# Experts' matrices in one ring of five places, with context's work spread earlier over the experts

## The reference

```python
def expert_block(args):
    xb, e = args
    hdn = jax.nn.silu(xb @ w1[e]) * (xb @ w3[e])      # w1, w3: 1024 x 512, 32 experts
    return hdn @ w2[e]                                # w2: 512 x 1024
...
proj_c = hc @ w_ctx                                   # hc: the context, normed and modulated; w_ctx: 1024 x 2560
kc = rms_norm_2(proj_c[..., :GQA_KV_WIDTH].reshape(B, L, GQA_KV_HEADS, GQA_HEAD_DIM), p["k_norm"])
vc = proj_c[..., GQA_KV_WIDTH:GQA_CTX_COLS].reshape(B, L, GQA_KV_HEADS, GQA_HEAD_DIM)
...
oc = gqa_attend(qc, kc, vc).reshape(B, L, GQA_WIDTH)
yc = (oc * jax.nn.silu(gc)) @ p["w_out"]
```

## Time and profile before

| | us |
|---|---|
| median of 3 runs (lowest, highest) | 2011.4 (2009.6, 2015.0) |
| the profiled execution | 2020.8 |
| its span | 2018.7 |
| TensorE busy | 1821.2 (90% of the span) |
| VectorE, ScalarE busy | 753.6, 540.1 |
| DMA, mean over the span | 165 GB/s |
| the experts' loop, first SiLU to last output | 453 to 1025 |

### The profile page before, as it was taken

How to read it: one execution, slowest core, us unless ns; L and a number is a source line. 1 busy time by engine, 2 the same in 40 slices (tenths; PEclk the granted TensorE clock), 3 DMA queues, 4 the chain that set the end, 5 groups by cost and what they waited for, 6 DMA issues and landing times. The chain is left out here.

```text
span 2018.7 us, 24057 instructions
## 1 busy us (share of the span) xinstructions
PE 1821.2 (90%) x9644; PEld 1007.6 (50%) x9644; DVE 753.6 (37%) x1471; ACT 540.1 (27%) x1110; POOL 148.2 (7%) x194
## 2 busy tenths in 40 slices
PE   8999878988788989999869999899998999699998
PEld 3333455454344434446445444566645544466663
DVE  2333576131124111134323314566423225555542
ACT  2111476110110011133214212444311232234430
POOL 2110000000111101110000014000000001100000
PEclk9999899979898989999989999999998999899999
DMA  7655927249999999999671222000200011000001
GB/s 264 217 184 184 190 33 100 112 176 415 403 390 388 412 398 388 401 375 354 262 280 70 83 83 83 1 1 1 97 0 32 21 57 63 22 1 2 1 22 42
DMA packets 91950, 333.44 MB, mean 165 GB/s; under 512 B 10112, under 2 KB 26624, under 8 KB 64832
## 3 DMA queue, kind: packets, MB, share of 16 engines
q1 hardware_dynamic: 73376, 247.64, 34.8%
q10 hardware_dynamic: 13264, 67.22, 8.8%
q0 software_dynamic: 5200, 17.04, 2.1%
HBM read 317.58 MB, written 14.30 MB: 164 GB/s over the span
## 5 line engine op out<-in xcount | busy, mean ns | idle before, releaser
L1015 PE MATMUL mix_ps<-arena 128*64 128x256 f32 x2048 | 238.1, 386 | 2.5 <-DVE arena L1510 2.5
L2031 PE MATMUL tail_ps<-arena 128*128 128x512 f32 x504 | 219.6, 592 | 0.0
L1027 PE MATMUL mix_ps<-arena 128*64 128x512 f32 x512 | 145.2, 719 | 66.9 <-DMA arena<-in_w 66.3
L1015 PEld LDWEIGHTS mix_ps<-arena 128*64 128x64 f32 x2048 | 143.3, 138 | 89.1 <-issue 20.2
L903 PE MATMUL mix_ps<-arena,side 128*128 128x512 f32 x384 | 175.3, 609 | 1.4 <-DVE side L1335 1.4
L443 DVE TENSOR_REDUCE tail_small<-tail_ps 128x1 f32<-128x768 f32 x128 | 116.6, 953 | 137.7 <-PE tail_ps L327 137.7
L2031 PEld LDWEIGHTS tail_ps<-arena 128*128 128x128 f32 x504 | 95.0, 190 | 114.8 <-issue 114.3
L903 PEld LDWEIGHTS mix_ps<-arena,side 128*128 128x128 f32 x384 | 72.1, 194 | 103.4 <-issue 85.2
L2031 PE MATMUL tail_ps<-arena,side 128*128 128x512 f32 (+2 forms) x320 | 122.1, 543 | 0.0
L526 ACT ACTIVATE arena<-tail_ps,tail_small 128x768 f32<-128x768 f32 x128 | 113.8, 899 | 3.7 <-DVE tail_small L443 3.7
L1027 PEld LDWEIGHTS mix_ps<-arena 128*64 128x64 f32 x512 | 40.6, 164 | 147.6 <-issue 77.2
(11 more groups left out here) (373 smaller groups left out, 2323.7 us busy)
## 6 DMA issues: line engine op xcount, KB each, us to landing
arena<-in_w SPq DMA_DIRECT2D x66, 2048.0 KB, 12.0
arena<-in_w ACTq DMA_DIRECT2D x30, 2048.0 KB, 10.6
arena<-in_l_w_in SPq DMA_DIRECT2D x22, 1024.0 KB, 7.4
arena<-in_l_w_mod SPq DMA_DIRECT2D x16, 1024.0 KB, 5.0
arena<-in_w_in SPq DMA_DIRECT2D x12, 1024.0 KB, 9.3
arena<-in_l_w_mod SPq DMA_DIRECT2D x16, 512.0 KB, 4.5
residual<-bias_blocks SPq DMA_DIRECT2D x32, 224.0 KB, 10.1
arena<-in_l_w_out SPq DMA_DIRECT2D x6, 1024.0 KB, 5.1
```

The lines of the kernel that those rows point to most:

```text
L1015: last = pe.matmul(out[h * CAP:(h + 1) * CAP, 0:H2], x, wb[:, k, h * H2:(h + 1) * H2], start=(k == 0), stop=(k == DK - 1))
L1027: last = pe.matmul(py[h * CAP:(h + 1) * CAP, :], x, wb[:, f, h * 512:(h + 1) * 512], start=(f == 0), stop=(f == FK - 1))
L2031: last = pe.matmul(out, lhs(k), rhs(k), start=(k == 0), stop=(k == K - 1))
```

## The change

The five places become one ring for all three kinds of matrix, in the order in which TensorE uses them: w1(0), w3(0), then w1(e+1), w3(e+1), w2(e) and so on, so that use q lies in place q % 5 and may be loaded when use q - 5 is done. For w2(e) that is h1(e); ScalarE asks for it behind silu(e). SP asks for w1(e+2) when h3(e) is done and for w3(e+2) when second(e-1) is done. The six pieces of context's columns are asked for by ScalarE too, in experts 9, 11, ... 19. Context's product goes from experts 12 to 23 to experts 9 to 20, its steps from three an expert from 24 on to two an expert from 21 on, the small work on modulation, gates, side and overflow into experts 1 to 6. The three matrices of the last expert have places of their own in the ring. Two of the four "cg" pieces are loaded in the second block.

```diff
-    w1b = [view(proj_w, 0, DK, D_EXPERT), view(ring, SLOT, DK, D_EXPERT)]
-    w3b = [view(proj_w, 4096, DK, D_EXPERT), view(ring, 3 * SLOT, DK, D_EXPERT)]
-    w2b = view(proj_w, 8192, D_EXPERT // P, D)
+    matrix_at = [view(proj_w, 0, 4096), view(proj_w, 4096, 4096), view(ring, SLOT, 4096), view(ring, 3 * SLOT, 4096), view(proj_w, 8192, 4096)]
+    use_of = lambda which, e: dict(w1=3 * e - 1 if e else 0, w3=3 * e if e else 1, w2=3 * e + 4)[which]
+    one_of = lambda q: [("w1", 0), ("w3", 0)][q] if q < 2 else [("w3", q // 3), ("w2", (q - 4) // 3), ("w1", (q + 1) // 3)][q % 3]
+    used = lambda which, e: (s[dict(w1="h1", w3="h3", w2="y")[which]], e + 1)
+    late_at = dict(w1=(matrix_at[2], used("w3", STATIC - 2)), w3=(matrix_at[3], used("w2", STATIC - 3)), w2=(matrix_at[1], used("w2", STATIC - 2)))
...
             def expert(e, which):
-                w, buf = dict(w1=(A["w1"], w1b), w3=(A["w3"], w3b))[which]
-                if e >= 2:
-                    sp.wait_ge(s[dict(w1="h1", w3="h3")[which]], e - 1)
-                sp.dma_start(runs(buf[e % 2]), w[e].rearrange("(a p j) n -> p a (j n)", a=2, p=P)).then_inc(s[which][e % 2], 16)
+                q = use_of(which, e)
+                if q >= 5:
+                    sp.wait_ge(*used(*one_of(q - 5)))
+                sp.dma_start(runs(matrix_at[q % 5]), A[which][e].rearrange("(a p j) n -> p a (j n)", a=2, p=P)).then_inc(s["w"][q % 5], 16)
...
-                if e in range(13, 25, 2):
-
-                    i = (e - 13) // 2
-                    sp.wait_ge(*((s["c_mm"], 2 * i) if i else (s["over_indexed"], 1)))
-                    sp.dma_start(piece, src_c[:, 4 * (i % 2):4 * (i % 2) + 4, 512 * (i // 2):512 * (i // 2 + 1)]).then_inc(s["c_in"], 16)
...
                 if e >= C_FIRST:
-                    context_step(3 * (e - C_FIRST))
+                    context_step(2 * (e - C_FIRST))
...
-                if e in range(12, 24):
-                    context_product(e - 12)
+                if e in range(9, 21):
+                    context_product(e - 9)
...
                 act.activation(sact, p1[:, 0:H2], ACT.Silu).then_inc(s["silu_done"], 1)
+                if e:
+
+                    q = use_of("w2", e)
+                    assert one_of(q - 5) == ("w1", e)
+                    act.dma_start(matrix_at[q % 5].rearrange("p (a n) -> p a n", a=2), A["w2"][e].rearrange("(a p j) n -> p a (j n)", a=2, p=P)).then_inc(s["w"][q % 5], 16)
+                if e in range(9, 21, 2):
+
+                    i = (e - 9) // 2
+                    act.wait_ge(*((s["c_mm"], 2 * i) if i else (s["over_indexed"], 1)))
+                    act.dma_start(piece, src_c[:, 4 * (i % 2):4 * (i % 2) + 4, 512 * (i // 2):512 * (i // 2 + 1)]).then_inc(s["c_in"], 16)
...
                 if e:
-
                     outputs(e - 1)
-                    act.dma_start(w2b.rearrange("p (a j) n -> p a (j n)", a=2), A["w2"][e].rearrange("(a p j) n -> p a (j n)", a=2, p=P)).then_inc(s["w2"], 16)
...
+    plan("cg", 1, 2, None, l0_in, 2048)
     plan("p", 0, 4, None, plg_w, 0)
```

More of the change, by code:

```diff
@@ L557 @@
 OVER = 2 * SEQ // CAP
-C_FIRST = 24
+C_FIRST = 21
 class Weights:
@@ L836, in _ @@
             sp.wait_ge(s["listed"], 1)
-            sp.dma_start(runs(w2b), A["w2"][0].rearrange("(a p j) n -> p a (j n)", a=2, p=P)).then_inc(s["w2"], 16)
+            expert(0, "w2")
             for b in range(2):
@@ L847, in _ @@
                 expert(e, "w3")
-                if e in range(13, 25, 2):
-                    i = (e - 13) // 2
-                    sp.wait_ge(*((s["c_mm"], 2 * i) if i else (s["over_indexed"], 1)))
-                    sp.dma_start(piece, src_c[:, 4 * (i % 2):4 * (i % 2) + 4, 512 * (i // 2):512 * (i // 2 + 1)]).then_inc(s["c_in"], 16)
             sp.wait_ge(s["over_indexed"], 1)
-            p = STATIC % 2
             with sp.Fori(0, sp.value_load(trips_over, min_val=1, max_val=OVER + 1)) as i:
                 e = sp.value_load(experts_over[:, ds(i, 1)], min_val=0, max_val=N_EXPERTS - 1)
-                for w, wb, got, done, before, n in ((A["w1"], w1b[p], "w1", "h1", "h1", STATIC - 1), (A["w3"], w3b[p], "w3", "h3", "h3", STATIC - 1), (A["w2"], w2b, "w2", "y", "y", STATIC)):
-                    sp.wait_ge(s[before], n)
+                for which, done in (("w1", "h1"), ("w3", "h3"), ("w2", "y")):
+                    to, free = late_at[which]
+                    sp.wait_ge(*free)
                     sp.wait_ge(d[done], FIRST + i)
[L860 to L865, removed]
+                    sp.dma_start(runs(to), A[which][ds(e, 1)].rearrange("x (a p j) n -> p (x a) (j n)", a=2, p=P)).then_inc(d[which], 16)
+            src_c = A["l0_w_in"].rearrange("(k p) n -> p k n", p=P)
+            sp.wait_ge(*used("w3", STATIC - 1))
+            for z in range(2):
+                sp.dma_start(view(arena, z * SLOT, 4, 512), src_c[:, 4 * z:4 * z + 4, 1536:2048]).then_inc(ring_in[z], 16)
         @block.tensor
@@ L999, in spread_gate @@
                 g, row = gate_rows[n]
-                if n:
-                    pe.wait_ge(s["mod_added"], n)
-                pe.matmul(ps[:, 6], m["ident"][:, row:row + 1].to_broadcast([P, P]), mod_rows[g], start=True, stop=True).then_inc(s["mod_spread"], 1)
+                if n >= 2:
+                    pe.wait_ge(s["mod_added"], n - 1)
+                pe.matmul(ps[:, 6 + n % 2], m["ident"][:, row:row + 1].to_broadcast([P, P]), mod_rows[g], start=True, stop=True).then_inc(s["mod_spread"], 1)
             def turn_rows(buf, sem, n, done):
@@ L1086, in context_step @@
                     g = w // 2
[L1087 to L1091, removed]
+                    for kt in range(2):
+                        for x in range(2):
+                            last = pe.matmul(ps[64 * x:64 * x + 64, 6, 0:2 * P], cproj[:, kt, 256 + 64 * g:256 + 64 * (g + 1)],
+                                             pTc[:, :, (2 * x + kt) * P:(2 * x + kt + 1) * P], start=(kt == 0), stop=(kt == 1))
                     last.then_inc(s["ctx_pv"], 1)
@@ L1685, in _ @@
                     dve.tensor_tensor(ctx_in[:, t], ctx_in[:, t], mods[0][1][:, XT + t].unsqueeze(2).to_broadcast([P, DK, P]), ALU.add).then_inc(s["ctx_gained"], 1)
+                if e == 4:
+                    dve.wait_ge(s["sd_s"], 2)
+                    chain(inverse_root(dve, chain, ss_s, sd_s, D, half_s, rs_s))
+                    dve.wait_ge(s["side_gain"], 16)
+                if e in (4, 5):
+                    for t in (2 * e - 8, 2 * e - 7):
+                        of_tile = view(side, 0, XT, D)[:, t]
+                        chain(dve.scalar_tensor_tensor(out=of_tile, in0=of_tile, scalar=rs_s[:, t:t + 1], in1=side_gain, op0=ALU.mult, op1=ALU.mult))
+                if e == 4:
+                    overflow()
+                if e == 6:
+                    overflow_listed()
+                if e in range(8, 8 + len(tables)):
+                    scale_tables(dve, chain, tables[e - 8:e - 7])
             take_hidden(STATIC - 1)
@@ L1907, in ring_piece @@
         due[key] = (ring_in[i], seen[i])
-    for n in range(2):
-        for z in range(2):
-            ring_piece(("cg", n, z), 2 * n + z)
+    for z in range(2):
+        ring_piece(("cg", 0, z), z)
     ring_plan = []
@@ L1977, in _, with load_y @@
         def _(sp):
-            for t in range(XT):
+            def load_y(t):
                 sp.dma_start(y_of[t], ys[0:2 * SEQ, :].rearrange("(x t p) d -> t p x d", p=P, x=2)[t]).then_inc(s["y_in"][t], 16)
+            for t in range(2):
+                load_y(t)
             for key, i, free, src in ring_plan:
+                if key == ("p", 0, 0):
+                    for t in range(2, XT):
+                        load_y(t)
                 if free is not None:
```

125 lines of the change are left out of this document (59 added, 66 removed).

## The result

| | us, median (lowest to highest) |
|---|---|
| before, 4 runs | 2011.5 (2009.6 to 2015.0) |
| changed, 4 runs | 2048.0 (2046.9 to 2049.5) |
| ratio | 1.0158, 95% interval 1.0128 to 1.0188 |
| profiled execution after, its span | 2047.3, 2045.2 |

The change makes the kernel 36.5 us slower; +13 was forecast, with 2046 as the upper end. The direction and the place were right, the size was not.

A forecast was written before the change was run, and what follows sets the result against it. The experts' loop was taken as bound by transfers up to 816 us and by TensorE in context's steps. -8 + 50 - 22 - 7.5 + 0.5 = +13 us gave 2024 us in the median, range 1996 to 2046.

The forecast's parts named there:

- Context's pieces: silu(9) to silu(21): each piece lands 19.0 us after the SiLU, TensorE waits, a pair takes 44.6 us; +50 us.
- rival (b): Context's pieces: every run takes its turn whatever its size, pairs of 48 us, total 2043; chance 0.15 with beyond.
- rival (a): Context's pieces: bytes are shared evenly, pairs of 41.8 us, total 2007, no change; chance 0.20 together with another rival.
- Early experts: silu(2) to silu(9): ring and earlier w2 request remove short gaps in the stream; -8 us (ends 0 and -12).
- Context's steps: silu(21) to silu(30): steps spread over nine experts instead of six, 149 us against 171.3; -22 us.
- The end of the loop: second(30): w2(30) asked for at silu(30), about 2 us of its 8.03 us wait stay; -7.5 us.
- Second block: Two "cg" pieces loaded ahead of y's second half, all still in time; +0.5 us, 5 if the cover failed.
- Rival (c): Context's pieces: ScalarE's queue hardly held up, loop transfer-bound, pairs of 36.2 to 38 us, sum -38 to -27; chance 0.19.

The follow-up runs named there:

- the run with early pieces: Against the changed kernel, ScalarE asks for context's six pieces one expert sooner, at the end of experts 8, 10, ... 18: 1971.9 us, ratio 0.9778.

## Why the prediction was half right

**Context's pieces: the step that failed.** Forecast +50, measured +80.9. The mechanism (the piece stands behind w2(e) on ScalarE's queue, its runs of 2 KB against SP's, and the expert's own end uses it) held in each of six pairs. The wrong term is the landing, "w2 at 11.0 us, the piece in 8.0": in five pairs w2 took 11.3 to 13.4 and the piece 11.3 to 12.3, so it landed 23.6 to 24.7 us after the SiLU instead of 19.0; in the first pair w2 took 15.7, the piece 13.5, and it landed at 29.2. Together the six are 35.2 us late, and most of it is the piece: 8.0 us was put for it, 11.3 to 13.5 it took. The rest of the pair was right: in the second pair 10.35 us from the product's start to the next SiLU against 7.36 + 2.7, and the even expert 15.5; over all six it gave 4 us back, and 31 was missing from the forecast. The upper bound of 11.3 us for the piece was its lowest value, and rival (b), with 48 us a pair and 2043, is what happened.

I leaned on one landing of before, 6.6 us behind its forerunner, and read it wrong. A piece is not moved between its forerunner's landing and its own: in the trace of before this one's 512 packets start from 647.7 to 658.2, 10.6 us, though its forerunner landed at 652.2. Nor was it alone at the end: of the 0.54 MB of 657.5 to 658.8 only 0.04 are its own, the rest is SP's next matrix. So the pace of 11.2 us was about right and the 6.6 was not a time of the piece. The trace of before also had the rule. From 651 to 654.5 us, with w2 in runs of 8 KB on ScalarE's queue (q10) and the piece on SP's (q1):

```profile
q10 hardware_dynamic: 109, 0.89, 61.1%
q1 hardware_dynamic: 109, 0.23, 16.6%
```

Packet for packet, and four bytes to one. So the argument for rival (a) from this same w2 fails: its queue did have four fifths of what the two moved. The sentence that no row tells a packet's size was wrong for the same reason: the page's line of packets, the same for both kernels, counts runs. And the gather that was brought for rival (b) has packets of 4 KB in the trace, not of 2.

**Early experts.** Forecast -8 with -12 as the far end, measured -14.2. The stream went to 420 GB/s, worth the 6.5 us of the rate; the granted clock is 0.95 against 0.89, with fewer waits for w2, so the sum was too careful. The work moved to experts 1 to 6 costs 1.7 us, in silu(0) to silu(2). The experiments put it on the ring (123.9 us without it) together with w2's early request (148.5 without that).

**Context's steps.** Forecast -22, TensorE's own sum of 147 us; measured 146.85. The transfers did not hold it back: they ran at 418 GB/s, and I had taken 406.

**The end of the loop.** -7.5 against -11.2. w2(30) lands 9.8 us after silu(30) and its wait is 0.65 us instead of 8.03, and the wait ahead of the second block is 12.8 instead of 15.1, which I had taken as fixed. Part of this is luck: in the run with early pieces, where the stream is full up to here, w2(30) lands at 14.3 us and the stretch gains only 4.0.

**Second block.** +0.5 against +3.2: the gate's pieces are in time as argued, but y's second half is needed sooner than I took it; the row of the changed kernel has 2.7 us of waiting for VectorE, whose additions wait for y.

**The sum.** The pieces were 31 us dearer than forecast and the second block 3, the other three stretches together 12 us cheaper, so that the total is off by less than the term that failed.

Rival (c) asked where the piece lands; with it in place early (the run on ScalarE, one expert sooner) context's stretch is bound by the transfers and the time is 45 us below its own runs of before (2016.5), where (c) gave 27 to 38.

## What to carry to other kernels

When several queues feed the same DMA engines, price a transfer by its runs: in this case a queue beside a full one got own run / (own run + theirs) of the rate until that one was empty, and a landing close behind the forerunner's was no sign of a fast transfer. Count the packets of each queue in the stretch instead; ask for transfers in short runs early, or put them ahead of the long ones on their queue. A ring of places and the moment of each request belong together: if two requests hang on one event, they share the rate, and a request that hangs on the use of its forerunner turns its landing time into the loop's period. Work bound by one engine is best spread over work bound by the transfers, since either alone leaves the other idle.

## What was not expected of the hardware

- Two queues that are both full move one run each in turn (324 packets to 323, 191 to 190, 109 to 103), so that the share of a queue follows the length of its runs: 0.18, 0.31 and 0.50 of the rate for 2, 4 and 8 KB beside 8 KB, for transfers of the same bytes.
- The stream from memory ran at 418 to 420 GB/s for 110 and 147 us on end with both hardware queues in use (399 before): the 2% that looked like a full engine hid 5% of rate.
